# Strassen's seven products for an encoder layer's gate and up projections, in two passes of 1024 tokens

## The chip, the cores and the metric

The kernel runs on one core of one Trainium2 chip. The metric is the device time of one execution in microseconds (us), the median of several runs. A core has five engines that run side by side, each with its own instruction stream, and wait for each other by semaphores: TensorE (PE), VectorE (DVE), ScalarE (ACT), GpSimd (POOL) and SyncE (SP, which only issues transfers here). SBUF is the on-chip memory of 128 partitions, PSUM holds TensorE's results in 8 banks of 128 x 512 fp32.

## The reference

The layer has 2048 tokens of width 1024. After the mixers (windowed attention and a state-space branch) it ends like this:

```python
x = x + rmsnorm(merged @ w_out, norm_mix_post)
h2 = rmsnorm(x, norm_ffn_pre)
gate = h2 @ w_ffn_gate                      # 1024 -> 2816
up = h2 @ w_ffn_up                          # 1024 -> 2816
gp = jnp.pad(gate, ((0, 0), (1, 1), (0, 0)))
gate = gp[:, :-2] * conv_w[0] + gp[:, 1:-1] * conv_w[1] + gp[:, 2:] * conv_w[2] + conv_b
f = jax.nn.gelu(gate) * up
return x + rmsnorm(f @ w_ffn_down, norm_ffn_post)
```

Everything is fp32 in and out.

## The kernel before, in words

The kernel is a row of stages, each in its own block, with a barrier of all engines between them; what passes from one to the next goes through DRAM. In order: projection in, mixers, branches, output projection (`stage_out`, tiles named `ou_`), gate and up (`stage_gate_up`, `gu_`), down projection (`stage_down`, `dn_`).

Every large product is made of three fp32r matmuls (`split_products`, lines 324 to 326): both operands are split into a high part, rounded to fp32r, and a low part, the rest; high x high, low x high and high x low are added up in one PSUM bank. A split is one copy (the high part) and one subtraction (the low part), whose two inputs both lie in SBUF.

`stage_out` works through 16 tiles of 128 tokens. For each, SP loads 128 tokens of `merged`, ACT makes the high part and DVE the low part, PE does 48 matmuls (8 k, 2 halves of the width, 3 products). ACT then squares the result, POOL computes the inverse root in four small operations, DVE scales the rows and adds the residual, and POOL stores them to `x_mid`.

`stage_gate_up` starts with `NormTranspose`: SP loads 16 tiles of rows of `x_mid`, ACT squares, POOL makes the inverse root, DVE scales, PE transposes each tile in 8 pieces (line 253), and ACT (line 213) and DVE (line 234) keep the high and low parts of all 2048 tokens in SBUF. From the second group of four tiles on, the first block's product runs between the transposes. Then follows a loop over 22 row blocks of 128 of the 2816, each once for gate and once for up. `WeightStream` loads 128 columns of weights (512 KB), and DVE splits them (lines 314 and 316). PE computes four chunks of 512 tokens, each in its own bank, 24 matmuls to a bank. ACT copies gate's banks out (line 518), DVE runs the three taps of the convolution over 2048 tokens (lines 539, 542, 545), ACT applies gelu (line 522), DVE multiplies with up's banks (line 553), and POOL issues the store of the row block to `f` (line 571). ACT loads a function table each time it changes between copy and gelu. The four loads of the taps and the bias (lines 507 and 508) are the first things in ACT's stream. POOL has nothing in the loop but the 22 stores.

The order of work on each engine is the order of its code; nothing is planned at run time. PE's wait before a block is for the weights' low part, and before a bank for the one who reads it.

Of the kernel before, what the change touches and what calls it, by code (L numbers as in the profile page):

```python
# [28 lines left out]
P = 128  # L29
# [414 lines left out]
def stage_gate_up(nc, x_mid, gain, w_gate, w_up, conv_w, conv_b, f_scratch):  # L444


    with ExitStack() as ctx:
        m = Pool(nc, ctx, "gu")
        nt = NormTranspose(m, x_mid, gain)
        m.sb("shift", [P, 96])  # L450
        ws = WeightStream(m, KD)

        gate = m.sb("gate", [P, TOK + 2])
        conv = m.sb("conv", [P, TOK])
        taps = m.sb("taps", [P, 4, KF])
        banks = m.psum("banks", [P, 8, BANK])
        turn_psum = banks[:, 4:8, :].rearrange("p (s b) (k t) -> p s (b k) t", s=2, t=P)
        taps_in = m.sem("taps_in")
        edges_zero = m.sem("edges_zero")
        gate_read = m.sem("gate_read")  # L460
        up_read = m.sem("up_read")
        gate_free = m.sem("gate_free")
        tap = m.sem("tap")
        gelu_done = m.sem("gelu_done")
        stored = m.pool_dma_sem("stored")
        conv_free = m.sem("conv_free")
        f_rows = f_scratch.rearrange("(b p) t -> b p t", p=P)
        block = ctx.enter_context(nc.Block())

        @block.gpsimd  # L470
        def _(pool):
            pool.memset(gate[:, 0:1], 0.0).then_inc(edges_zero, 1)
            pool.memset(gate[:, TOK + 1:TOK + 2], 0.0).then_inc(edges_zero, 1)
            nt.gpsimd(pool)

        @block.sync
        def _(sync):
            nt.load(sync, ws, [(s, weights, slice(0, P)) for s, weights in enumerate((w_gate, w_up))])
            with sync.Fori(1, KF) as i:
                ws.load(sync, w_gate, 0, i * 2, bass.ds(i * P, P))  # L480
                ws.load(sync, w_up, 1, i * 2 + 1, bass.ds(i * P, P))

        @block.tensor
        def _(pe):
            def product(i, s):
                pe.wait_ge(ws.lo_ready, i * 2 + s + 1)
                for c in range(CHUNKS):

                    pe.wait_ge(up_read if s else gate_read, i * CHUNKS + c + 1)
                    for k in range(KD):  # L490
                        cols = slice(c * BANK, (c + 1) * BANK)
                        last = split_products(pe, banks[:, s * CHUNKS + c, :], ws.hi[:, s, k], ws.lo[:, s, k],
                                              nt.feat_hi[:, k, cols], nt.feat_lo[:, k, cols],
                                              k == 0, k == KD - 1)
                    last.then_inc(ws.chunk_done, 1)

            nt.tensor(pe, turn_psum, banks, ws)
            product(0, 1)
            with pe.Fori(1, KF) as i:
                for s in range(2):  # L500
                    product(i, s)

        @block.scalar
        def _(act):
            with nc.allow_non_contiguous_dma(reason="small"):
# [3 lines left out]
            nt.scalar(act, turn_psum)  # L509
            act.sem_inc(gate_read, CHUNKS)  # L510
            act.sem_inc(gelu_done, 1)
            act.wait_ge(taps_in, 64)
            with act.Fori(0, KF) as i:

                act.wait_ge(gate_free, i + 1)
                for c in range(CHUNKS):
                    ws.wait_chunk(act, i * 2, c)
                    act.activation(gate[:, 1 + c * BANK:1 + (c + 1) * BANK], banks[:, c, :], ACT.Copy)\  # L518
                        .then_inc(gate_read, 1)

                act.wait_ge(tap, i * 3 + 3)
                act.activation(conv[:], conv[:], ACT.Gelu_apprx_tanh, bias=taps[:, 3, bass.ds(i, 1)])\
                    .then_inc(gelu_done, 1)

        @block.vector
        def _(dve):
            nt.vector(dve, turn_psum, ws)
            dve.sem_inc(gate_free, 1)
            dve.sem_inc(up_read, CHUNKS)
            dve.wait_ge(taps_in, 64)  # L530
            dve.wait_ge(edges_zero, 2)
            dve.sem_inc(conv_free, 1)

            def finish(i):


                dve.wait_ge(gate_read, i * CHUNKS + 2 * CHUNKS)
                dve.wait_ge(conv_free, i + 1)
                dve.tensor_scalar(conv[:], gate[:, 0:TOK], taps[:, 0, bass.ds(i, 1)], None,
                                  ALU.mult).then_inc(tap, 1)  # L540
                dve.wait_ge(tap, i * 3 + 1)
                dve.scalar_tensor_tensor(out=conv[:], in0=gate[:, 1:TOK + 1], scalar=taps[:, 1, bass.ds(i, 1)],
                                         in1=conv[:], op0=ALU.mult, op1=ALU.add).then_inc(tap, 1)
                dve.wait_ge(tap, i * 3 + 2)
                dve.scalar_tensor_tensor(out=conv[:], in0=gate[:, 2:TOK + 2], scalar=taps[:, 2, bass.ds(i, 1)],
# [1896 lines left out]
```

## Time and profile before

| | us |
|---|---|
| median of the runs | 3066.26 (3 runs, 3066.14 to 3066.8) |
| span of the profiled execution | 3065.0 (no other time is given for that execution) |
| PE busy | 2799.5 (91%) |
| DVE busy | 1266.1 (41%) |
| ACT busy | 760.4 (25%) |
| POOL busy | 530.8 (17%) |
| output projection, from block start to the next | 1326.7 to 1526.7 |
| gate and up: start to last matmul | 1526.7 to 2545.1 |
| down projection | 2553.6 to the end |

The span goes from the first to the last instruction of one execution. Busy time of PE is drawn with each matmul's drain, so neighbouring matmuls overlap in the rows: what one costs is the distance between two starts. Stage borders are read from the first instruction of the next block.

### The profile page before, as it was taken

The numbers are of one execution on the slowest core, as the hardware profiler recorded it, in microseconds if no ns is written. First come the engines' busy times: TensorE is split into PE (matmuls) and PEld (weight loads), VectorE is DVE, ScalarE is ACT, GpSimd is POOL, SyncE is SP. The second block draws the span as 40 slices with busy tenths as digits, with TensorE's granted clock in tenths as the row PEclk, the third lists the DMA queues.
The fourth block names the chain that finished last, engine by engine and source line by source line (L and its number), as shares of the span: only waits on it lengthen the run. The fifth ranks groups of instructions, "written<-read, shape, count | busy, mean of one in ns | idle before, by whom it ended". The sixth has DMA issues, their size and how long they took to land. (4 is left out here: it accounts for less than half of the span.)

```text
span 3065.0 us, 35647 instructions
## 1 busy us (share of the span) xinstructions
PE 2799.5 (91%) x12942; PEld 2293.0 (75%) x12942; DVE 1266.1 (41%) x1448; ACT 760.4 (25%) x1200; POOL 530.8 (17%) x840
## 2 busy tenths in 40 slices
PE   6996999778988879979759999999999997999998
PEld 5885788666877667868648888888888885888886
DVE  5013664598696065433253232322223223224432
ACT  4111665522222150022141111111111113113221
POOL 2363220188880000001120000000000001000111
PEclk9997999899999989989979999999999998999999
DMA  5551324645555653355341111111111106334553
GB/s 158 161 203 57 75 66 101 176 150 157 186 175 191 119 195 139 149 172 144 118 129 55 34 55 48 55 34 55 48 54 38 51 34 199 94 98 146 170 169 118
DMA packets 375392, 350.66 MB, mean 114 GB/s; under 512 B 49552, under 2 KB 322960, under 8 KB 366480
## 3 DMA queue, kind: packets, MB, share of 16 engines
q1 hardware_dynamic: 326560, 227.93, 26.1%
q0 software_dynamic: 14352, 76.03, 6.9%
q10 hardware_dynamic: 34400, 45.67, 4.5%
q8 instruction: 47, 0.77, 0.1%
q14 instruction: 33, 0.27, 0.0%
HBM read 242.09 MB, written 107.48 MB: 114 GB/s over the span
## 5 line engine op out<-in xcount | busy, mean ns | idle before, releaser
L324 PE MATMUL gu_banks<-gu_feat_hi,gu_w_hi 128*128 128x512 f32 (+1 forms) x1408 | 549.8, 390 | 1.0 <-DVE gu_feat_lo L234 1.0
L326 PE MATMUL gu_banks<-gu_feat_lo,gu_w_hi 128*128 128x512 f32 (+1 forms) x1408 | 548.8, 390 | 0.0
L325 PE MATMUL gu_banks<-gu_feat_hi,gu_w_lo 128*128 128x512 f32 (+1 forms) x1408 | 548.5, 390 | 0.0
L324 PEld LDWEIGHTS gu_banks<-gu_feat_hi,gu_w_hi 128*128 128x128 f32 x1408 | 264.9, 188 | 55.7 <-DVE gu_feat_lo L234 1.4
L326 PEld LDWEIGHTS gu_banks<-gu_feat_lo,gu_w_hi 128*128 128x128 f32 x1408 | 264.8, 188 | 55.1
L325 PEld LDWEIGHTS gu_banks<-gu_feat_hi,gu_w_lo 128*128 128x128 f32 x1408 | 264.9, 188 | 54.6
L324 PE MATMUL dn_y<-dn_w_hi,dn_f_hi 128*128 128x512 f32 x704 | 276.1, 392 | 22.7 <-DVE dn_w_lo L815 22.6
L314 DVE CAST gu_w_hi<-gu_w_raw 128x1024 fp32r<-128x1024 f32 x44 | 30.5, 694 | 619.2 <-PE gu_banks L326 619.2
L325 PE MATMUL dn_y<-dn_w_hi,dn_f_lo 128*128 128x512 f32 x704 | 275.4, 391 | 0.0
L326 PE MATMUL dn_y<-dn_w_lo,dn_f_hi 128*128 128x512 f32 x704 | 275.2, 391 | 0.0
L518 ACT ACTIVATE gu_gate<-gu_banks 128x512 f32<-128x512 f32 x88 | 52.7, 601 | 596.3 <-PE gu_banks L326 596.2
L571 POOL DMA_DIRECT2D f<-gu_conv x22 | 11.8, 536 | 936.5 <-DVE gu_conv L553 936.5
L324 PEld LDWEIGHTS dn_y<-dn_w_hi,dn_f_hi 128*128 128x128 f32 x704 | 132.9, 189 | 52.5 <-issue 19.4
L326 PEld LDWEIGHTS dn_y<-dn_w_lo,dn_f_hi 128*128 128x128 f32 x704 | 133.1, 189 | 27.9
L325 PEld LDWEIGHTS dn_y<-dn_w_hi,dn_f_lo 128*128 128x128 f32 x704 | 133.1, 189 | 27.6
L2352 POOL TENSOR_TENSOR bases<-gs_states,bases 128x512 f32<-128x512 f32 (+2 forms) x90 | 109.6, 1218 | 202.9 <-POOLq L2373 179.6
L2238 ACT ACTIVATE gs_w_hi<-gs_w_raw 128x1024 fp32r<-128x1024 f32 x64 | 67.9, 1060 | 302.6 <-PE gs_banks L326 284.3
L763 ACT ACTIVATE dn_f_hi<-dn_f_raw 128x1408 fp32r<-128x1408 f32 x64 | 85.2, 1372 | 204.0 <-PE dn_y L326 163.0
L2272 DVE TENSOR_TENSOR gs_w_lo<-gs_w_raw,gs_w_hi 128x1024 fp32r<-128x1024 f32 x64 | 104.3, 1629 | 74.1 <-ACT gs_w_hi L2238 74.0
L324 PE MATMUL gs_banks<-gs_feat,gs_w_hi 128*128 128x512 f32 x256 | 104.8, 410 | 26.0 <-DVE gs_w_lo L2272 26.0
L324 PE MATMUL pi_banks<-pi_feat_hi,pi_w_hi 128*128 128x512 f32 (+1 forms) x320 | 126.2, 394 | 1.0 <-DVE pi_feat_lo L234 1.0
L326 PE MATMUL pi_banks<-pi_feat_lo,pi_w_hi 128*128 128x512 f32 (+1 forms) x320 | 125.1, 391 | 0.0
(259 smaller groups left out, 5066.7 us busy)
## 6 DMA issues: line engine op xcount, KB each, us to landing
dn_f_raw<-f SPq DMA_DIRECT2D x64, 704.0 KB, 5.7
gs_w_raw<-in_w_in SPq DMA_DIRECT2D x64, 512.0 KB, 4.5
f<-gu_conv POOLq DMA_DIRECT2D x22, 1024.0 KB, 4.2
gates<-gs_gate_out ACTq DMA_DIRECT2D x64, 256.0 KB, 3.0
br_rows<-gates POOLq DMA_DIRECT2D x16, 1024.0 KB, 6.9
gu_w_raw<-in_w_ffn_gate SPq DMA_DIRECT2D x22, 512.0 KB, 3.8
gu_w_raw<-in_w_ffn_up SPq DMA_DIRECT2D x22, 512.0 KB, 3.9
dn_w_raw<-in_w_ffn_down POOLq DMA_DIRECT2D x22, 512.0 KB, 6.0
```

The source lines that it names most:

```text
L314: dve.tensor_copy(self.hi[:, s], self.raw[:, s]).then_inc(self.hi_ready, 1)
L324: pe.matmul(out, w_hi, x_hi, start=first, stop=False)
L325: pe.matmul(out, w_lo, x_hi, start=False, stop=False)
L326: return pe.matmul(out, w_hi, x_lo, start=False, stop=last)
L518: act.activation(gate[:, 1 + c * BANK:1 + (c + 1) * BANK], banks[:, c, :], ACT.Copy)\
L571: pool.dma_start(f_rows[i], conv[:]).then_inc(stored, 16)
L763: act.activation(f_hi[:, s, h * KH:(h + 1) * KH], f_raw[:, h], ACT.Copy)\
L2238: act.activation(w_hi[:, n % 2], w_raw[:, n % 2], ACT.Copy).then_inc(w_hi_ready, 1)
L2272: dve.tensor_tensor(w_lo[:, n % 2], w_raw[:, n % 2], w_hi[:, n % 2].bitcast(F32), ALU.subtract)\
L2352: engine.tensor_tensor((by_re, by_im)[n], source, factor, ALU.mult).then_inc(done, 1)
```

## The change

The gate and up products are made by one level of Strassen's scheme, in Winograd's form. The weights of a pair of row blocks (256 columns) are cut into four quarters, A11 to A22, of 512 rows of k by 128 columns; the features of 1024 tokens into four, of 512 of k by 512 tokens. Seven products of 4 k x 3 matmuls give the four 128 x 512 results, where eight would be needed. For the weights POOL makes four sums and differences, two in place; for the features it makes 16 differences of 128x512, in place. SBUF has no room for the seven split right operands of all tokens, so the stage runs in two passes of 1024 tokens, each over 11 pairs and over gate and up: 44 units. The weights are loaded once in each pass.

The seven results share four banks of each kind: product 0 and 4 bank A, 1 and 5 bank C, 2 and 6 bank DD, 3 bank B; the later product of a bank is added to the earlier, after ACT has copied the earlier one out (products 0 and 1), or DVE has read it (product 2).

```diff
+HALF = TOK // 2
+KHALF = KD // 2
+PAIRS = KF // 2
+PER_PASS = 2 * PAIRS
+UNITS = 2 * PER_PASS
+OPS = 7
...
+            def product(u, j):
+                bank = banks[:, kind, (A, C, DD, B, A, C, DD)[j]]
+                pe.wait_ge(a_lo_ready, u * OPS + j + 1)
...
+                if j == 4:
+                    pe.wait_ge(p_one_kept, u + 1)
+                if j == 5:
+                    pe.wait_ge(p_five_kept, u + 1)
+                if j == 6:
+                    pe.wait_ge(u_three_ready, u + 1)
+                for k in range(KHALF):
+                    if u % PER_PASS == 0:
+                        pe.wait_ge(b_lo_ready, (p * OPS + j) * KHALF + k + 1)
+                    last = added_products(pe, bank, a_hi[:, j, k], a_lo[:, j, k], b_hi[:, j, k], b_lo[:, j, k],
+                                          j < 4 and k == 0, k == KHALF - 1, j >= 4)
```

POOL's stream (each difference of features waits for the split of what it overwrites, and the split of its result waits for it):

```diff
+            sum_one(0)
+            sum_three(0)
+            for k in range(KHALF):
+                difference_one(0, k)
+            sum_two(0)
+            for k in range(KHALF):
+                difference_three(0, k)
+            sum_four(0)
+            for k in range(KHALF):
+                difference_two(0, k)
+            for k in range(KHALF):
+                difference_four(0, k)
+            for u in range(UNITS):
+                turning = u == PER_PASS - 1
+                if u + 1 < UNITS:
+                    sum_one(u + 1)
+                    sum_three(u + 1)
...
+                if u % 2:
+                    times_up(u, 1, 1)
+                    times_up(u, 0, 1)
+                    up_edge(u)
+                    times_up(u, 1, 0)
+                if turning:
+                    for k in range(KHALF):
+                        difference_four(1, k)
```

ACT's stream (copies of products 0 and 1, gelu of one row block at a time, high parts):

```diff
+            for j in range(OPS):
+                split_a(0, j)
+                split_b(0, j)
             act.wait_ge(taps_in, 64)
+            for u in range(UNITS):
+                for j in range(OPS):
+                    if j == 0:
+                        keep_one(u)
+                    if j == 1:
+                        keep_five(u)
+                    if u % 2 and j in (3, 4):
+                        gelu(u, j - 3)
+                    if u % 2 == 0 and j == 4:
+                        keep_c11(u)
+                    if u + 1 < UNITS:
+                        split_a(u + 1, j)
+                    if u == PER_PASS - 1:
+                        split_b(1, j)
```

DVE's stream (low parts, the sums of the results, convolution of 1023 or 1025 columns for each of two row blocks):

```diff
+            for u in range(UNITS):
+                up, turning = u % 2 == 1, u == PER_PASS - 1
+                if up:
+                    convolve(u, 0)
+                split_a(u + 1, 0)
+                if turning:
+                    split_b(1, 0)
+                if up:
+                    convolve(u, 1)
+                split_a(u + 1, 1)
+                if turning:
+                    split_b(1, 1)
+                split_a(u + 1, 2)
+                u_two_three(u)
...
+                c22(u)
+                if up:
+                    up_c11(u)
+                split_a(u + 1, 4)
...
+                c12(u)
+                split_a(u + 1, 5)
...
+                c21(u)
+                if not up:
+                    edges(u)
+                split_a(u + 1, 6)
```

`split_a` is one operation of 128x512, `split_b` four of them. SP loads the weights by halves of k (512 KB each, a ring of three) and also issues the stores to `f` (1 MB, two row blocks of 1024 tokens). All of the stage's code is written out, without loops.

`stage_out` takes over the FFN's norm and transposes. For each tile, after the residual sum, ACT squares the rows, POOL makes three small operations, DVE scales (`norm_mid`), and PE transposes the tile two tiles later; ACT keeps the first 1024 tokens in SBUF (`feat_raw`), which stays for the next stage, and copies the others out and stores them to DRAM (`feat_late`), from where they are loaded in the first pass:

```diff
+            sync.dma_start(mid_gain[:], row_broadcast(ffn_gain)).then_inc(mid_gain_in, 16)
...
+            for t in range(TILES):
+                tile(t)
+                if t >= 2:
+                    turn_tile(t - 2)
+            turn_tile(TILES - 2)
+            turn_tile(TILES - 1)
...
+            for t in range(TILES):
+                act.wait_ge(y_done, t + 1)
+                pn.scalar(act, t, t % 2, [y[:, t % 2, 0], y[:, t % 2, 1]])
+                if t + 2 < TILES:
+                    split_hi(t + 2)
+                square_mid(t)
+                if t >= 2:
+                    keep_features(t - 2)
```

## Rows read from the trace of the kernel before

**Rows 1.** The page, part 1: busy us (share of the span) and instructions.
```profile
PE 2799.5 (91%) x12942; PEld 2293.0 (75%) x12942; DVE 1266.1 (41%) x1448; ACT 760.4 (25%) x1200; POOL 530.8 (17%) x840
```

**Rows 2.** Windows of gate/up: length, busy PE, PEld, DVE, ACT, POOL; PEclk, DMA, GB/s.
```profile
1526.70:1564.80 38.10, 8.82 (x40) 7.34 (x41) 14.16 (x12) 10.54 (x16) 7.63 (x25) 0.54 0.69 167
1564.80:1607.00 42.20, 34.15 (x177) 27.24 (x176) 28.73 (x24) 23.94 (x33) 9.36 (x30) 0.92 0.31 100
1607.00:2545.10 938.10, 938.08 (x4139) 776.70 (x4137) 266.58 (x237) 152.05 (x154) 11.26 (x21) 1.00 0.14 46
```

**Rows 3.** Timeline of PE (start, length): gate/up, 48 matmuls apart; mixers, 111 apart.
```profile
1730.28 0.39 PE L324 MATMUL gu_banks<-gu_feat_hi,gu_w_hi 128*128 128x512 f32 x1
1741.16 0.39 PE L324 MATMUL gu_banks<-gu_feat_hi,gu_w_hi 128*128 128x512 f32 x1
...
799.45 0.39 PE L324 MATMUL gs_banks<-sm_u_region,gs_w_hi 128*128 128x512 f32 x1
824.61 0.39 PE L324 MATMUL gs_banks<-gs_feat,gs_w_hi 128*128 128x512 f32 x1
```

**Rows 4.** Groups of instructions: count, busy us, mean ns, idle before and its releaser.
```profile
L316 DVE TENSOR_TENSOR br_w_lo<-br_w_raw,br_w_hi 128x512 fp32r<-128x512 f32 x20 | 13.8, 692 | 0.7
L1119 ACT ACTIVATE ou_g_hi<-ou_g_raw 128x1024 fp32r<-128x1024 f32 x16 | 16.9, 1056 | 185.8 <-DMA ou_g_raw<-merged 185.8
L522 ACT ACT_TABLE_LOAD x22 | 28.2, 1283 | 177.5 <-DVE gu_conv L545 177.5
L539 DVE TENSOR_SCALAR gu_conv<-gu_gate,gu_taps 128x2048 f32<-128x2048 f32 x22 | 28.3, 1286 | 26.1 <-ACT gu_gate L518 17.6 <-DVE gu_w_lo L316 8.4
L542 DVE SCALAR_TENSOR_TENSOR gu_conv<-gu_gate,gu_taps,gu_conv 128x2048 f32<-128x2048 f32 x22 | 51.7, 2352 | 3.2 <-DVE gu_conv L539 3.2
```

**Rows 5.** Timeline of POOL and DVE in the mixers; last, one group by form.
```profile
281.96 2.02 POOL L1434 TENSOR_TENSOR at_table_temp<-bases 128x1024 f32<-128x1024 f32 x1
639.99 4.30 DVE L2352 TENSOR_TENSOR bases<-gs_states,bases 128x512 f32<-128x512 f32 x2
645.73 1.82 DVE L2272 TENSOR_TENSOR gs_w_lo<-gs_w_raw,gs_w_hi 128x1024 fp32r<-128x1024 f32 x1
648.92 1.36 POOL L2352 TENSOR_TENSOR bases<-gs_states,bases 128x512 f32<-128x512 f32 x1 [0.18 <-POOL bases L2352]
654.38 1.83 DVE L2272 TENSOR_TENSOR gs_w_lo<-gs_w_raw,gs_w_hi 128x1024 fp32r<-128x1024 f32 x1
...
L2352 DVE TENSOR_TENSOR bases<-gs_states,bases 128x512 f32<-128x512 f32 x30 | 52.3, 1745 | 0.7
```

**Rows 6.** Timeline of ACT's queue: the last of its four loads of taps.
```profile
1541.02 2.06 ACTq L508 DMA_DIRECT2D gu_taps<-in_conv_b  x1
```

**Rows 7.** The page, part 6: transfers, KB each, median us from issue to landing.
```profile
dn_f_raw<-f SPq DMA_DIRECT2D x64, 704.0 KB, 5.7
f<-gu_conv POOLq DMA_DIRECT2D x22, 1024.0 KB, 4.2
gates<-gs_gate_out ACTq DMA_DIRECT2D x64, 256.0 KB, 3.0
gu_w_raw<-in_w_ffn_gate SPq DMA_DIRECT2D x22, 512.0 KB, 3.8
```

**Rows 8.** Timeline of PE: one of the first matmuls of gate/up.
```profile
1565.38 0.63 PE L325 MATMUL gu_banks<-gu_feat_hi,gu_w_lo 128*128 x1
```

**Rows 9.** Timeline of PE's weight loads: one tile's eight transposes.
```profile
1600.17 0.85 PEld L253 LDWEIGHTS gu_banks<-gu_ident,gu_normed 128*128 128x128 f32 x8 [1.49 <-issue]
```

**Rows 10.** Timeline at the ends of the output projection and of gate/up.
```profile
1519.49 1.23 DVE L644 TENSOR_TENSOR ou_rows<-ou_rows,ou_scaled 128x1024 f32<-128x1024 f32 x1
1526.79 0.33 SPq L163 DMA_DIRECT2D gu_rows<-x_mid  x1
...
2544.69 0.39 PE L326 MATMUL gu_banks<-gu_feat_lo,gu_w_hi 128*128 128x512 f32 x1
2553.59 1.13 SPq L698 DMA_DIRECT2D dn_f_raw<-f  x2
```

More of the change, by code:

```diff
@@ L441, in _, with added_products @@
                 act.wait_ge(stored[s], (n_blocks // 2) * 16 + 16)
-def stage_gate_up(nc, x_mid, gain, w_gate, w_up, conv_w, conv_b, f_scratch):
+HALF = TOK // 2
[4 more added lines that the diff above has]
+OPS = 7
+def added_products(pe, out, w_hi, w_lo, x_hi, x_lo, first, last, again):
+    pe.matmul(out, w_hi, x_hi, start=first, stop=False, skip_group_check=again)
+    pe.matmul(out, w_lo, x_hi, start=False, stop=False, skip_group_check=again)
+    return pe.matmul(out, w_hi, x_lo, start=False, stop=last, skip_group_check=again)
@@ L470, in _, with wait_raw @@
         @block.gpsimd
         def _(pool):
[L472 to L481, printed above, removed]
+            def wait_raw(u, h):
+                n = 2 * u + h
+                pool.wait_ge(raw_in[n % 3], n // 3 * 16 + 16)
@@ new lines, in keep_five, with keep_c11 @@
+            def keep_five(u):
+                act.wait_ge(product_done, u * OPS + 2)
+                if u:
+                    act.wait_ge(c22_done, u)
+                act.activation(p_five[:], banks[:, u % 2, C], ACT.Copy).then_inc(p_five_kept, 1)
+            def keep_c11(u):
+                _, _, g = place(u)
+                act.wait_ge(product_done, u * OPS + 5)
+                if g:
+                    act.wait_ge(tap, g * 6)
+                act.activation(out_of(u, 0, 0), banks[:, 0, A], ACT.Copy).then_inc(gate_c11_done, 1)
@@ L505, in _, with gelu @@
+            def gelu(u, e):
+                p, pair, g = place(u)
+                act.wait_ge(tap, g * 6 + 3 * e + 3)
+                size = HALF - 1 + 2 * p
+                act.activation(conv[:, e, 0:size], conv[:, e, 0:size], ACT.Gelu_apprx_tanh,
+                               bias=taps[:, 3, 2 * pair + e:2 * pair + e + 1]).then_inc(gelu_done, 1)
             with nc.allow_non_contiguous_dma(reason="small"):
@@ new lines, in convolve @@
+            def convolve(u, e):
+                p, pair, g = place(u)
+                if e == 0:
+                    dve.wait_ge(gate_c11_done, g + 1)
+                    dve.wait_ge(edge_kept, g + 1)
+                    if g:
+                        dve.wait_ge(stored, g * 16)
+                size = HALF - 1 + 2 * p
+                out = conv[:, e, 0:size]
+                weight = [taps[:, j, 2 * pair + e:2 * pair + e + 1] for j in range(3)]
+                first = g * 6 + 3 * e
+                dve.tensor_scalar(out, gate[:, e, 0:size], weight[0], None, ALU.mult).then_inc(tap, 1)
+                for j in range(1, 3):
+                    dve.wait_ge(tap, first + j)
+                    dve.scalar_tensor_tensor(out=out, in0=gate[:, e, j:j + size], scalar=weight[j], in1=out,
+                                             op0=ALU.mult, op1=ALU.add).then_inc(tap, 1)
@@ L530, in _ @@
+            for j in range(OPS):
+                split_a(0, j)
+                split_b(0, j)
             dve.wait_ge(taps_in, 64)
             dve.wait_ge(edges_zero, 2)
[L532 to L545, printed above, removed]
-                                         in1=conv[:], op0=ALU.mult, op1=ALU.add).then_inc(tap, 1)
@@ L1103, in tile, with turn_tile @@
                 done.then_inc(y_done, 1)
-            pe.sem_inc(y_done, 2)
-            tile(0, 0, first=True)
-            tile(0, 1)
-            with pe.Fori(1, TILES // 2) as i:
-                for s in range(2):
-                    tile(i, s)
+            def turn_tile(t):
+                s = t % 2
+                pe.wait_ge(mid_ready, t + 1)
+                if t >= 2:
+                    pe.wait_ge(feat_copied, t - 1)
+                for k in range(KD):
+                    turn = pe.transpose(turn_psum[:, s, k, :], mid_normed[:, s, k * P:(k + 1) * P], ident[:])
+                turn.then_inc(turned, 1)
```

481 lines of the change are left out of this document (363 added, 118 removed).

## The prediction, made before the changed kernel was run

> **What bounds the kernel now.** I read the page's engine totals first: PE multiplies 2799.5 us of 3065.0 (91%); DVE, next after PE's own weight loads, has 41% on the page [rows 1]. The reader is to see there that only fewer matmuls, or fewer holes between them, can move the time. Next the windows by stage: from 1607 to 2545 us, the gate/up loop, PE has 938.08 busy us in 938.10 at granted clock 1.00 with DVE at 28%, ACT at 16% and POOL at 1%; before it stand 38.1 us in which PE does 8.8 and 42.2 in which it does 34 [rows 2]. Then the timeline of PE inside the loop: two matmuls 48 places apart start 10.88 us apart, so one costs 0.2267 us whatever its own row says (0.39, drawn with its drain) [rows 3]. The chain that ended last shows only the down projection, so it decides nothing here. In this loop time is the count of matmuls times 0.2267, as long as the others keep up; that is what the rest asks.
>
> **The products.** Before: 44 blocks x 4 banks x 8 k x 3 = 4224 matmuls. After: 44 units (22 pair-halves of gate and up, two passes) x 7 products x 4 k x 3 = 3696. One unit is 84 x 0.2267 = 19.04 us, a product 2.72 us. The code of PE is now straight-line; in the gate products of the mixers, whose code is too, 111 matmuls take 25.16 us, 0.2267 each [rows 3]: I take 0 for it.
>
> **Does an ordinary unit keep PE fed?** Prices [rows 4]: the low part of a 128x512 split on DVE 0.69, and I take the same for an add or a product of 512 columns; the high part on ACT 0.57 (1.056 for 1024 columns, and half the columns leave a little over half), a PSUM copy 0.6 and a gelu of 1024 columns 1.1 at the same rate, a table load 1.28, taps of 1025 columns 0.7 and twice 1.28 (from 1.286 and 2.352 for 2048), semaphore gaps 0.15. A gate unit costs DVE 7 splits and 5 adds, 8.3 us; an up unit adds the two convolutions (7.1) and one product: 16 us. ACT has 5.9 and, with two gelus and four table loads, 13.2. All below 19.04. The splits of unit u+1 follow unit u's product of the same number, 16 us ahead of their use. The tight wait is the seventh product, which takes the bank of product 3 only when U3 has been added. In an up unit DVE does, from its start: C21 and the edge of the unit before (1.1), a split (1.8), convolution (5.3), split, convolution (9.6), two splits (11.0), U2 and U3: 12.6 us; the product wants it at 6 x 2.72 = 16.3. Waiting behind that pair on DVE are four splits and C22, and POOL's products behind C22; none is wanted for 10 us. ACT's keep copies run at 2.7 and 5.4 us, wanted at 10.9 and 13.6.
>
> What can eat the 3.7 us is POOL. It gets 8 sums and 3 products of 128x512 in two units, which nobody did there before. The trace has such a neighbourhood: while the scan runs on POOL, two 128x512 adds on DVE take 4.30 us instead of 1.38 (1.745 is their mean over the stage); POOL's 1024 columns alone take 2.02, so 512 about 1.05. From one gs_w_lo to the next (645.73 to 654.38) the two engines' work without company, about 3.3 and 4.6 us, fills 8.65 [rows 5]. They take turns. In the up unit two of POOL's sums fall ahead of U3: 2 x 1.3 puts it at 15.2. Margin 1.1 us; the unit holds. The Trainium skill, "SBUF — State Buffer", section "Who interferes with whom", has the rule: a VectorE instruction with two SBUF inputs and a GpSimd instruction that reads SBUF exclude each other for the whole instruction. The trace agrees (0.69 becomes about 2.0, the price of both in turn); by the rule alone a contested pair would cost 0.69 + 1.05 = 1.74, and the prologue below would be 5 us shorter.
>
> **The start of the stage.** Before: stage start 1526.72, last matmul done at 2545.1: 1018.4 us. ACT issues the four tap loads first, to 1543.1 [rows 6]; they stay first, so its first split comes 16.4 us in, with the weights (3.8 us landing [rows 7]) long there. Then all seven right operands are made: 28 + 7 splits on ACT (20 us) and DVE, and 16 + 2 in-place differences on POOL that each wait for a split and are waited for by one. Contested: 18 x 2.0 = 36, and 17 splits more at 0.69 = 11.7; from 17.2 to about 65 us. The fifth product waits for ACT's keep copy, which is queued behind the last of ACT's 35 splits, and the seventh for U3, behind the last of DVE's and three more: 65 + 2.1 + 1.4 = 68.5, and 2.7 for the product. Unit 0 ends 72 us in. Ends: 50 if the two engines don't exclude each other (POOL's chain alone, 18 x 1.2 from 18.6 on, then two splits, the keep copy and three products, with 2 us for gaps), 82 if each of its handovers costs twice the 0.15 us.
>
> **The turn of the passes.** In unit 21 the 28 splits and 16 differences come again, among the unit's own. DVE reaches U3 of unit 21 after 11 splits and both convolutions, with ten of POOL's operations between: about 31 us in, wanted at 16.3: 15 us. Then the order of POOL: its last four differences stand behind unit 21's last product with up, which waits for C21 on DVE, behind 15 more splits: they end near 55 us, the last split of ACT behind them, and behind that the keep copy of unit 22, which its fifth product wanted at 45.6: 11 to 12 us. I take 27 in all; 12 without exclusion, 40 at the other end. Reloading the late features (4 MB on SP's queue, issued at half-tile 10 of 88) has hundreds of us. After the idle start of the old stage the granted clock is 0.54 in the mean [rows 2], near 1.2 of 2.4 GHz, and the first matmuls are drawn with 0.63 instead of 0.39 [rows 8]; for such restarts I take 2 us together.
>
> New stage, start to last matmul: 72 + 43 x 19.04 (818.7) + 27 + 2 = 919.7 against 1018.4: **98.7 less**.
>
> **The output projection.** PE is paced there as well: tiles of 48 matmuls, 10.88 us. Eight transposes take 0.86 us until the next matmul [rows 9]; 13 tiles' worth fall before the last tile ends: 11.2 us more. DVE's added norm (1.28) and ACT's square and copy (2.3) leave both under 6 us of 11.8 a tile. The gain row is 512 KB more on SP's queue while the weights still arrive and ACT waits for them: 1.5 (0 to 3). At the end, before: sum done 1520.7, store issued, next stage 1526.7 [rows 10]. After: square 1.25, POOL's three steps 1.2, norm 1.28, transposes 2 (at the lower clock), copy 1.03, then 512 KB to DRAM with 512-byte runs, 4.5 (3.0 for 256 KB, 5.7 for 704 KB [rows 7]), and the barrier as before, 1.3: 1533.5, so 7 more (5 to 9). The input DMAs, waiting in SP's queue for the rows of two tiles earlier, have 15 us to spare. **19.7 more.**
>
> **The end of gate/up.** After the last matmul now: product 0.69, store on POOL, landing 4.2, next stage at 2553.6 [rows 7, 10]. After: C21 0.69, POOL's product 1.1, SP's issue of the same 1 MB: **1.2 more**.
>
> **Sum.** -98.7 + 19.7 + 1.2 = -77.8 us. The span is 3065.0; the profile has no other time for its execution, and the median of the runs shown is 3066.26, 1.3 above the span. 3066.3 - 77.8 = 2988.5: **2988.5 us**, 2.5% faster.
>
> **Rivals.** (a) *Engines don't exclude each other here*: most of POOL's operands are contiguous and each short, and one of its scan operations of 512 columns took 1.36 [rows 5]. Start at 50, turn at 12: 37 us less, 2951. Against it: the 4.30 for two. 0.15. (b) *U3 late in up units*: if tensor_scalar of an odd length runs at one element a cycle (0.4 more each, twice) and a third contested pair falls in, U3 stands at 17.3 to 18.3: 1 to 2 us in each of 22 up units, 22 to 44 us: 3010 to 3033. For it: a margin of 1.1. Against: POOL's next sum waits for that very split. 0.17. (c) *DVE and POOL together become the bound, and it is slower than before*: two units give DVE 24 us of work, of which 16 instructions contend. At the scan's mean of 1.745 for each and the convolutions blocked as often, 45 us against 38.1: 7 us a pair, 22 pairs, +154: 3142. It decides against the change from 3.5 us a pair. Against it: POOL is busy 13 us in 38, not always as in the scan, so it can't block DVE for 21. 0.10. (d) *Start and turn far longer*, above 80 and 45, from a chain of waits I have not seen: 3020 to 3066. 0.05.
>
> **Chances.** Forecast 0.53, with a range of its own of 2968 to 3012 (the start's and turn's ends, in part cancelling); (a) 0.15, (b) 0.17, (c) 0.10, (d) 0.05. The range takes (a), the forecast and most of (b): 2948 to 3045. A change of 0.2%, 6 us, is what a measurement can tell from none. Slower is (c), 0.10; within 0.2% is the last part of (d), 0.02; faster is the rest, 0.88.
>
> **What would show it.** In the changed profile: matmuls of gate/up 0.2267 apart and 19.0 us from one unit's first to the next's; the first matmul 18 us after the stage's start and the eighth product 72 after it; POOL's 128x512 rows near 1.2 alone and 1.9 in the start; a hole of 15 us before unit 21's seventh product, waiting for DVE, and one of 11 before unit 22's fifth, waiting for ACT; the output projection 11 longer between first and last matmul. The forecast is wrong if PE has a hole in every up unit (then (b) or (c)), or if the start takes under 60 or over 85 us.

## The result, and the profile after

The changed kernel takes 2973.88 us (median of 4 runs, 2973.55 to 2974.55) against 3066.53 beside it: ratio 0.9698, interval 0.9684 to 0.9712, so 3.0% faster. Forecast were 2988.5, and 2948 to 3045 as the range. A hole, below, is idle time of PE just before a matmul.

The page, part 1, of the changed kernel (answers to [rows 1]): PE has 105 us less to do, DVE 371 and POOL 383 more.

```profile
PE 2694.6 (91%) x12414; PEld 2199.8 (74%) x12414; DVE 1636.8 (55%) x1950; ACT 933.3 (31%) x1565; POOL 913.8 (31%) x1111
```

Windows of the changed kernel: output projection (its first 5 us still belong to the stage before), unit 0, units 1 to 20, the turn, the second pass, the down projection (columns as in [rows 2]):

```profile
1326.70:1545.97 219.27, 191.80 (x896) 159.35 (x896) 90.70 (x89) 77.12 (x136) 43.02 (x133) 0.94 0.51 163
1545.97:1607.60 61.63, 35.09 (x84) 22.50 (x85) 49.47 (x45) 24.55 (x44) 39.58 (x26) 0.64 0.29 50
1607.60:2000.00 392.40, 392.40 (x1733) 324.92 (x1732) 279.52 (x332) 141.09 (x222) 163.52 (x125) 1.00 0.29 93
2000.00:2062.00 62.00, 39.20 (x156) 31.51 (x155) 56.55 (x58) 25.76 (x44) 40.77 (x27) 0.83 0.16 51
2062.00:2453.40 391.40, 391.40 (x1728) 323.79 (x1726) 271.93 (x326) 134.70 (x210) 154.54 (x121) 1.00 0.24 77
2453.40:2972.10 518.70, 483.07 (x2113) 398.08 (x2112) 180.33 (x151) 127.26 (x150) 44.76 (x106) 0.97 0.50 147
```

There are two kinds of stretch. In the third and the fifth PE is never idle at clock 1.00: 41 of the 44 units cost their matmuls and nothing else. In the second and the fourth DVE is busy 80% and 91% of the time and PE waits. All that PE waits for there (line, releaser: us in total, times, longest; 7.4 more stand in the output projection's tail):

```profile
PE gu_banks L454 <- DVE gu_b_lo L812: 24.6, 5, 18.0
PE gu_banks L454 <- issue: 14.5, 2, 10.8
PE gu_banks L454 <- DVE gu_gate L831: 12.0, 1, 12.0
PE ou_turn L1496 <- DVE ou_mid_normed L1570: 7.4, 1, 7.4
PE gu_banks L454 <- ACT gu_u_two L754: 3.5, 1, 3.5
```

The account, by starts. The output projection's first load is issued at

```profile
1327.84 1.00 SPq L1068 DMA_DIRECT2D ou_g_raw<-merged  x2
```

in the kernel before and at

```profile
1331.83 1.01 SPq L1436 DMA_DIRECT2D ou_g_raw<-merged  x2
```

in the changed one: +4.0 us from the stages ahead of it, whose code is the same in both. In the profiled executions of all the kernels of this document that issue lies between 1326.3 and 1332.9, so such a difference says nothing of the change. (The block begins at 1327.8, and not at 1326.7 as the table of the time before has it.) The output projection then takes 214.1 us against 199.0 (+15.2), and gate/up begins at 1545.97 against 1526.72 (+19.3 in all); from there to the last matmul 907.1 against 1018.0 (-110.9); from there to the down projection 7.8 against 8.9 (-1.1). Sum -92.7; the down projection takes 0.2 less, and the spans differ by 92.9 (3065.0 to 2972.1). Below, "stage" is the length from the stage's start to its last matmul in the profiled execution; times are compared by ratio to the kernel before on the same chip (3067 to 3068 there, so 0.001 is 3 us).

### The profile page after: what moved, and what is told of

The parts are those of the page before. It is cut to its first block and busy times, and to the rows that moved or that the text cites. A ratio compares the mean times of both kernels' runs of the same rounds, so it can differ in the third digit from the quotient of the medians.

```text
span 2972.1 us, 35255 instructions
## 1 busy us (share of the span) xinstructions
PE 2694.6 (91%) x12414; PEld 2199.8 (74%) x12414; DVE 1636.8 (55%) x1950; ACT 933.3 (31%) x1565; POOL 913.8 (31%) x1111
## 5 line engine op out<-in xcount | busy, mean ns | idle before, releaser
L454 PE MATMUL gu_banks<-gu_b_hi,gu_a_hi 128*128 128x512 f32 x1232 | 488.0, 396 | 54.7 <-DVE gu_b_lo L812 24.6
L456 PE MATMUL gu_banks<-gu_b_lo,gu_a_hi 128*128 128x512 f32 x1232 | 485.3, 394 | 0.0
L455 PE MATMUL gu_banks<-gu_b_hi,gu_a_lo 128*128 128x512 f32 x1232 | 485.1, 394 | 0.0
L454 PEld LDWEIGHTS gu_banks<-gu_b_hi,gu_a_hi 128*128 128x128 f32 x1232 | 234.6, 190 | 112.0 <-issue 39.4
L456 PEld LDWEIGHTS gu_banks<-gu_b_lo,gu_a_hi 128*128 128x128 f32 x1232 | 234.7, 191 | 50.0
L455 PEld LDWEIGHTS gu_banks<-gu_b_hi,gu_a_lo 128*128 128x128 f32 x1232 | 235.2, 191 | 48.1
L806 DVE TENSOR_TENSOR gu_a_lo<-gu_raw,gu_a_hi 128x512 fp32r<-128x512 f32 x220 | 199.8, 908 | 116.3 <-ACT gu_a_hi L738 116.3
L738 ACT ACTIVATE gu_a_hi<-gu_raw 128x512 fp32r<-128x512 f32 x220 | 138.6, 630 | 259.2 <-PE gu_banks L456 234.5
L880 DVE SCALAR_TENSOR_TENSOR gu_conv<-gu_gate,gu_taps,gu_conv 128x1023 f32<-128x1023 f32 (+1 forms) x88 | 134.1, 1524 | 3.1
L642 POOL TENSOR_TENSOR gu_conv<-gu_conv,gu_gate 128x512 f32<-128x512 f32 (+1 forms) x66 | 96.6, 1463 | 124.3 <-DVE gu_gate L837 58.9
```

The lines of the kernel that those rows point to most:

```text
L454: pe.matmul(out, w_hi, x_hi, start=first, stop=False, skip_group_check=again)
L455: pe.matmul(out, w_lo, x_hi, start=False, stop=False, skip_group_check=again)
L456: return pe.matmul(out, w_hi, x_lo, start=False, stop=last, skip_group_check=again)
L642: pool.tensor_tensor(mine, mine, factor, ALU.mult).then_inc(up_done, 1)
L738: act.activation(a_hi[:, j], a_source(u, j), ACT.Copy).then_inc(a_hi_ready, 1)
L806: dve.tensor_tensor(a_lo[:, j], a_source(u, j), a_hi[:, j].bitcast(F32), ALU.subtract)\
```

## The experiments

U2 and U3 are two sums that DVE makes one after the other: U2 from ACT's copy of product 0 and the bank of product 3, U3 from U2 and the bank of product 2. A unit's seventh product goes into that last bank, so it waits for U3.

The theory: an ordinary unit costs 84 x 0.2267; the whole gain is 528 matmuls less; the price stands in unit 0 and at the turn, where DVE and POOL take turns. The rivals were (a) no exclusion, (b) U3 late, (c) DVE and POOL as the bound, and that the gain comes from something else, the norm's move above all.

### Is it the matmuls? (e1_eighth_product)

```diff
-                for k in range(KHALF):
+                for k in [*range(KHALF)] * (2 if j == 3 else 1):
```

> Product 3 of every unit is computed twice (its bank starts anew), so a unit has 96 matmuls as four plain banks would; all else is the changed kernel's. Theory (an ordinary unit lasts as long as its matmuls): 44 x 12 x 0.2267 = 119.7 us more than the changed kernel's 2973.9, less up to 5 us that fall into the holes of the first unit: 3089 to 3094, slower than the kernel before. Rival (other engines set the pace of a unit, and the gain came from the shorter start): less than 60 us more, under 3034.

Measured 3086.68, ratio 1.0062 (1.0045 to 1.0079), stage 1020.1: 112.8 more than the changed kernel, which is 113.0 by the stage alone, and 2.3 below the range expected. With an eighth product the new scheme is slower than the kernel before. The 119.7 of the added matmuls are not all seen because some of them fill holes: those of the turn, of which the expectation had taken no account, shrink from 12.0 and 10.8 to 9.3 and 7.9, by a product's 2.72 each or a little more.

### What does the norm's move give alone? (e7_norm_alone, e7b_norm_alone)

Both have the eight products and loops of before; the features come ready from the output projection. They differ in one place of ACT's stream:

```diff
+            act.sem_inc(gate_read, CHUNKS)
+            act.sem_inc(gelu_done, 1)
             for c in range(CHUNKS):
...
-            act.sem_inc(gate_read, CHUNKS)
-            act.sem_inc(gelu_done, 1)
             act.wait_ge(taps_in, 64)
```

> One part alone: the output projection with the FFN's norm and transposes as in the changed kernel, and gate/up with four plain banks as before, fed from the kept and the stored features. Theory (the gain is the matmuls saved; moving the norm gives back most of what it takes): output projection 19 us longer, gate/up's start 60 us of lost time down to about 15 (taps 10.4, first splits 1.2, lower clock 2): 25 to 30 us less than before, 3036 to 3042. Rival (the norm's move carries the larger share of the 93 us): under 3020. Rival (it only costs): over 3066.

> Eight products as before the change, with the norm of the features made inside the output projection, as in e7_norm_alone; only the release of the PSUM banks of the gate (gate_read) now stands ahead of ScalarE's feature splits instead of behind them. Theory: in e7_norm_alone the first matmul waited 37.0 us in one hole for ScalarE's queue although its operands stood ready about 21 us earlier, so this order takes about 21 us off: 3034 to 3040 us, the first matmul of gate and up near 1553 and not at 1574, the stage from there as long as before. Against the kernel before that is 26 to 32 us faster by the move of the norm alone. Rival: the features' splits on VectorE, not the release, set the first matmuls, and the hole is broken into waits for feature splits of the same sum: 3050 to 3060 us.

The first missed: 3057.86, ratio 0.9972 (0.9962 to 0.9981). ACT released the PSUM banks only behind all its splits, and PE stood:

```profile
1574.28 0.77 PE L324 MATMUL gu_banks<-gu_feat_hi,gu_w_hi 128*128 128x512 f32 x1 [37.03 <-ACTq L525]
```

With the release ahead of the splits the same row is

```profile
1553.73 0.76 PE L324 MATMUL gu_banks<-gu_feat_hi,gu_w_hi 128*128 128x512 f32 x1 [16.24 <-DVE gu_feat_lo L552]
```

and the time 3038.82, ratio 0.9909 (0.9892 to 0.9925), as expected: the norm's move alone is worth 28 us, and Strassen's scheme the other 65 (each ratio is good to some 5 us). Its stage is 975.5; 957.5 of it are matmuls (4224 x 0.2267), 18 overhead. The changed kernel has 837.9 of matmuls and 69.2 of overhead. So the scheme takes off 119.7 and gives back 51 at the start and the turn.

### What do the differences cost? (e2_no_differences, e3_write_only)

e2 puts a semaphore increment in the place of each of POOL's 32 feature differences; e3 has in the first pass a `memset` of 1400 columns in the place of each (`pool.memset(conv...[:, 0:1400], 0.0)`), about as long (1.36 us from start to start), but reading nothing.

> POOL's 32 differences of features are left out (a semaphore increment stands in their place, so all waits and their order stay); the products are then of wrong operands. Theory (in the start and at the turn POOL's differences and DVE's splits exclude each other and add up): the start falls from 62 us to about 41 (35 splits on DVE 0.61 apart from 11 us on, then U2, U3 and a product), the turn's two holes of 12.0 and 10.8 us nearly vanish: 40 to 45 us less than 2973.9, 2929 to 2934. Rival (the start is set by ACT's and DVE's own splits, the differences lie beside them): 0 to 10 us less, 2964 to 2974.

> In the first pass each of the 16 differences of features is replaced by a memset of 1400 columns of a tile that is not in use yet: about as long on POOL (1.25 us) but reading nothing; the products of that pass are of wrong operands. Theory (exclusion by POOL's reading): DVE's splits in the start come down from 1.68 us apart to 0.61 where they have their inputs, POOL's rows from 1.7 to about 1.3 each, and the start is then POOL's chain: 62 us falls to 47 to 50, the whole to 2959 to 2962. Rival (POOL's chain of waits and its own speed set the start, DVE is only late behind it): POOL's rows stay near 1.7, time within 3 us of 2973.9.

e2: 2940.08, ratio 0.9589 (0.9573 to 0.9605), stage 874.6: 32.5 less, and short of the 40 to 45 expected. Unit 0 ends 46.2 us in and not 61.6, where 41 was meant; the two units of the turn last 47.9 us for 65.0, and 38.1 would be without any loss. e3: 2959.57, ratio 0.9650 (0.9634 to 0.9666), stage 896.5: 10.6 less, and the time as expected; all of it is at the start (unit 0 ends 51.2 us in, a little above the 47 to 50 expected; U3 of unit 0 at 47.5 us into the stage instead of 56.4), with the turn's holes unchanged at 12.0 and 10.9. POOL has about the same time to spend in e3; only its reads are gone. DVE's and POOL's rows of the changed kernel in unit 0, and DVE's for the same line in an unhindered stretch, show the price:

```profile
1564.04 6.79 DVE L812 TENSOR_TENSOR gu_b_lo<-feat_raw,gu_b_hi 128x512 fp32r<-128x512 f32 x4
1566.88 6.76 POOL L624 TENSOR_TENSOR feat_raw<-feat_raw 128x512 f32<-128x512 f32 x4
...
1597.48 2.48 DVE L812 TENSOR_TENSOR gu_b_lo<-feat_raw,gu_b_hi 128x512 fp32r<-128x512 f32 x4
```

From the start of such a row to the start of the next one on DVE (1570.76 and 1599.89, not shown) four pairs take 6.72 us, 1.68 a pair; alone four DVE operations take 2.40, 0.60 each. Rival (a) falls.

### Do the taps hold the start? (e4_taps_on_sync)

The four small loads leave the head of ACT's queue for SP's, behind the third load of weights:

```diff
                 load_half(n)
+                if n == 2:
+                    for j in range(3):
+                        sync.dma_start(taps[:, j, :], conv_w[j].rearrange("(b p) -> p b", p=P)).then_inc(taps_in, 16)
+                    sync.dma_start(taps[:, 3, :], conv_b.rearrange("(b p) -> p b", p=P)).then_inc(taps_in, 16)
```

> The changed kernel with the four small loads of the convolution's taps issued from SyncE's queue behind the third load of weights instead of from the head of ScalarE's queue. Theory: ScalarE spent its first 10.5 us of the stage on issuing them (8.4 and 2.0 us) and its first split began only then; now it begins at +6.5 or so (behind its wait for the operand), and since the operands of unit 0 set the end of unit 0, the stage is 3 to 6 us shorter: 2968 to 2971 us. Rival: VectorE's and GpSimd's pace (1.68 us for a pair that meets on their operands) sets the start, not ScalarE's first split: within 1.5 us of the changed kernel, 2972.5 to 2975 us. Third: SyncE's queue is held by the issue and loads of weights come late, slower by 2 us or more.

2968.5, ratio 0.9678 (0.9662 to 0.9694), against 0.9698: the intervals overlap, but the stage says it: 902.9, 4.2 less, as expected. ACT's first split starts 3.9 us in and not 10.5, the first matmul 6.0 and not 12.6 in; 4.7 of that is left at the end of unit 0; the rest goes into waits for DVE's splits.

### Is the turn a matter of order? (e5a_difference_four, e5b_both_holes)

```diff
                     for k in range(KHALF):
                         difference_two(1, k)
+                    for k in range(KHALF):
+                        difference_four(1, k)
                 if u % 2:
...
-                if turning:
-                    for k in range(KHALF):
-                        difference_four(1, k)
```

and in e5b, on DVE's stream:

```diff
                 split_a(u + 1, 0)
-                if turning:
-                    split_b(1, 0)
                 if up:
                     convolve(u, 1)
+                if turning:
+                    split_b(1, 0)
+                    u_two_three(u)
```

> The changed kernel with one move at the turn between the passes: GpSimd's difference for the fifth operand (the four rows of difference_four) stands ahead of its products with up instead of behind them. Theory: the second hole of the turn (10.8 us, ScalarE's keep copy behind its split of operand 6, which waits for that difference) goes, and part of the lower clock after it; the first hole (12.0 us, which waits for VectorE's gate of 2x2 sums, U3) stays: 11 to 13 us less than the changed kernel, 2961 to 2963 us. Rival: the hole only moves, since the products with up that are now later hold VectorE's convolution or the end of the unit: no less than 3 us gained, and a hole of 8 us or more on another releaser.

> The move of e5a_difference_four, and besides: at the turn VectorE makes the second convolution before its first split of the new pass, and the sum U3 right after that split; at the start of the stage ScalarE's two keep copies of unit 0 stand after its fourth split, and VectorE's sum U2/U3 of unit 0 after its fifth split, not behind all seven. Theory: both holes of the turn (12.0 and 10.8 us) and the clock lost behind them go, and 3 to 6 us of the start: 24 to 28 us less than the changed kernel, 2946 to 2950 us. Rival: the splits that are moved back become the late ones (a hole on a split of the new pass of 6 us or more at the turn): 2955 to 2963 us.

Both missed. e5a: 2970.05, ratio 0.9681 (0.9665 to 0.9697), stage 906.5. e5b: 2973.39, ratio 0.9692 (0.9676 to 0.9708), stage 908.6. The stage gains 0.6 us in e5a and loses 1.5 in e5b. What PE waits for after 2010 us, first in e5a, then in e5b:

```profile
2015.01 0.77 PE L454 MATMUL gu_banks<-gu_b_hi,gu_a_hi 128*128 128x512 f32 x1 [11.96 <-DVE gu_gate L830]
2037.37 0.76 PE L454 MATMUL gu_banks<-gu_b_hi,gu_a_hi 128*128 128x512 f32 x1 [5.72 <-DVE gu_a_lo L805]
2047.17 0.47 PE L454 MATMUL gu_banks<-gu_b_hi,gu_a_hi 128*128 128x512 f32 x1 [2.19 <-issue]
```

```profile
2013.94 0.76 PE L454 MATMUL gu_banks<-gu_b_hi,gu_a_hi 128*128 128x512 f32 x1 [2.50 <-DVE gu_b_lo L814]
...
2037.91 0.77 PE L454 MATMUL gu_banks<-gu_b_hi,gu_a_hi 128*128 128x512 f32 x1 [11.73 <-ACT gu_u_two L753]
2047.69 0.54 PE L454 MATMUL gu_banks<-gu_b_hi,gu_a_hi 128*128 128x512 f32 x1 [2.55 <-issue]
```

The holes are broken up and get new names, but their sum is still 20 us (19.9 in e5a; 20.3 in e5b with four short ones that are not shown; 22.8 in the changed kernel), and what is gained there is lost in matmuls at the lower clock: the two units of the turn, 38.1 us without loss, last 65.0 us in the changed kernel and in e5a, 65.6 in e5b. At the start, e5b's unit 0 ends 56.2 us in for 61.6, but a hole of 3.7 on U3 comes up in unit 1, and unit 2 begins 0.9 later than in the changed kernel. DVE is full meanwhile. e5a's window of the turn:

```profile
2000.00:2062.00 62.00, 42.12 (x156) 33.36 (x155) 59.98 (x58) 26.40 (x44) 40.84 (x26) 0.81 0.16 51
```

59.98 us of 62.00 (e5b has the same): here the turn lasts as long as DVE's work does, what POOL holds it up among it. In e2, where POOL has no differences, the holes there were 2.5 and 4.5. The releasers of the two holes were real, and moving what they waited for was worth nothing.

### Take work off that pair (e9a_differences_dve, e9b_all, e10_sum_first)

e9a moves the four `difference_*` functions from POOL's stream to DVE's, word for word, behind the split that each waits for (`differences(p, j)` is one and three behind split 0, two behind 1, four behind 3):

```diff
                 split_b(0, j)
+                differences(0, j)
...
                     split_b(1, 0)
+                    differences(1, 0)
```

e9b adds e4's taps and this order of DVE's turn, behind its first split and difference; besides, ACT's keep copies of unit 22 stand ahead of the split of operand 6, those of unit 0 behind the fifth split, U2/U3 of unit 0 behind the sixth:

```diff
+                    convolve(u, 1)
+                    split_a(u + 1, 1)
+                    u_two_three(u)
+                    for k in range(KHALF):
+                        difference_three(1, k)
+                    split_b(1, 1)
+                    differences(1, 1)
+                    split_a(u + 1, 2)
+                    split_b(1, 2)
+                    c22(u)
+                    up_c11(u)
+                    c12(u)
+                    c21(u)
+                    for j in range(3, OPS):
+                        split_a(u + 1, j)
+                        split_b(1, j)
+                        differences(1, j)
```

and e10 moves `u_two_three(22)` ahead of `split_a(23, 1)`.

> The changed kernel with the 32 differences of features (16 at the start, 16 at the turn) made by VectorE in its own queue, right behind the split that each waits for, instead of by GpSimd. Nothing is left out and nothing else is moved. Theory after e5a and e5b, where a hole of the turn only changed its place: VectorE is full there (59.98 of 62.00 us busy), and what sets both the start and the turn is its own work plus 1.08 us for each GpSimd difference that it meets (1.68 for the pair against 0.60 alone). A difference on VectorE costs 0.60, so 16 of them are about 8 us less of VectorE's time in each place, and what waits for them gets them sooner: the gate of 2x2 sums U3 of unit 0 at about 1590 and not 1602.4, the start 9 to 12 us shorter; the holes of the turn (22.8 us together) 8 to 14: in all 18 to 28 us less than the changed kernel, 2946 to 2956 us. Rival: the two engines do not hinder each other and VectorE's added 16 x 0.60 = 9.6 us per place come on top, 10 to 19 us slower: 2984 to 2993 us. Second rival: order and not VectorE's load sets the turn, then the start alone gives 9 to 12: 2962 to 2965 us.

> e9a_differences_dve and e4_taps_on_sync together, and an order of the turn made for VectorE's load: U2/U3 of unit 21 ahead of the second operand's split, its four outputs ahead of the fourth operand's split, ScalarE's two keep copies of unit 22 ahead of the split of operand 6; at the start the keep copies of unit 0 behind ScalarE's fifth split and U2/U3 of unit 0 behind VectorE's sixth. Theory: the taps' 4 to 5 us and some 4 to 8 us of the turn and start come on top: 2935 to 2945 us. If order does not matter: e9a less 5.

> e9b_all with one more move: in unit 22, the first after the turn, VectorE makes U2/U3 ahead of the second and third splits of the next unit's weights, not behind them. In e9b_all the last hole of the turn (8.4 us, on the gate of 2x2 sums U3) came because VectorE waited there for ScalarE's split of a weight sum that GpSimd got done only after a row of back-to-back VectorE operations, and U3 stood behind it. Theory: GpSimd's late sum no longer holds U3, which comes some 5 us sooner: 4 to 7 us less than e9b_all with the lower clock behind the hole, 2945 to 2949 us. Rival: the weight splits themselves are then late for unit 23 and the hole comes back there: within 2 us of e9b_all.

e9a: 2959.44, ratio 0.9654 (0.9638 to 0.9670), stage 893.8, 13.3 less: 7.4 at the start and 5.9 at the turn. The direction is the theory's (the rival "10 to 19 slower" falls), the size is not, and the time is 3.4 above the range expected. At the turn the holes are 9.9, 2.1 and 2.5, 14.5 together for 22.8. At the start U3 of unit 0 comes 50.6 us in for 56.4, where 44 was meant. What ate the rest, POOL and ACT in unit 0 of e9a:

```profile
1561.32 17.23 POOL L615 TENSOR_TENSOR gu_s_one<-gu_raw 128x512 f32<-128x512 f32 x1 [7.32 <-DVE gu_a_lo L765]
...
1578.58 0.63 ACT L697 ACTIVATE gu_a_hi<-gu_s_one 128x512 fp32r<-128x512 f32 x1 [9.32 <-POOL gu_s_one L615]
```

One sum of 1.26 us lies 17.23 us on POOL while DVE's rows follow one another without a gap (from 1561.09 to 1577.4). ACT waits 9.3 for it, with two splits and the keep copy behind it, and PE 11.1 for that copy. e9b: 2952.3, ratio 0.9624 (0.9608 to 0.9640), stage 886.5; above the 2945 expected, for the same cause: its last hole, 8.4 on U3, goes back to ACT waiting 9.6 for such a sum. e10 takes U3 out from behind it: that hole is 3.7, the stage 882.3, 4.2 shorter, as expected; the time, 2950.22, ratio 0.9621 (0.9605 to 0.9637), is 1.2 above the range and does not tell it from e9b. So order is worth something again here: in e9b's turn DVE is busy 53.2 us of 57.8, since it waits there, and in e10's 52.1 of 53.6. e10 beats both kernels: 3.8% less than before, 0.8% less than the changed one.

### How near was the bound? (e6_more_pool_work)

Four additions ahead of `sum_two`, as here, and three behind it:

```diff
+                if u % 2 and not turning:
+                    for n in range(0, 4):
...
+                        pool.tensor_tensor(spare[:], b_hi[:, 0, 0].bitcast(F32), b_hi[:, 0, 1].bitcast(F32), ALU.add)
```

> The changed kernel with seven more additions of 128x512 on GpSimd in each up unit but that of the turn (four ahead of sum_two, three behind it; they read b_hi and write a tile that nobody reads): work added, nothing left out. It asks how near the ordinary units were to the bound by VectorE and GpSimd. Theory: an addition costs both engines 1.68 us where they meet, U3 of an up unit comes at about 21 us where it is wanted at 16.3, so each of 21 up units gets a hole of 3 to 6 us: 63 to 126 us more than the changed kernel, 3037 to 3100 us, about the time before the change. Rival: GpSimd takes the idle time of VectorE (280 of 392 us busy) and U3 does not move by more than its slack of 3.6 us: 2972 to 2978 us.

3090.74, ratio 1.0080 (1.0063 to 1.0097), stage 1027.2, 120.1 more: slower than the kernel before, though before the addition POOL was busy 42% and DVE 71% of the ordinary units (third window above). Twenty of the 21 up units with additions get a hole on U3 (the stage's last unit has none); the second of them, and the windows behind the first:

```profile
1669.00 0.77 PE L454 MATMUL gu_banks<-gu_b_hi,gu_a_hi 128*128 128x512 f32 x1 [3.64 <-DVE gu_gate L846]
```

```profile
1624.20:1630.30 6.10, 6.10 (x15) 4.81 (x16) 5.81 (x7) 1.23 (x2) 3.52 (x3) 0.51 0.30 89
1630.30:1662.00 31.70, 31.70 (x141) 26.25 (x140) 20.98 (x22) 10.47 (x18) 20.11 (x15) 1.00 0.51 183
```

The twenty holes are 74.4 us. The rest of the 120 is the clock: behind the first, which ended at 1624.20, PE runs 6.1 us at the granted 0.51 (1.2 of 2.4 GHz), 3.0 us lost, nearly the hole again. Not behind every one: two up units are 38.08 us apart without holes, and the first ten holes lie 44.80 to 41.98 apart, so that 0.3 to 3.1 us are lost behind each, 2.3 on the average, which makes 46 of the 120. Rival (c) is a real mechanism; it just had not been reached.

## Why the prediction was right

**Products and ordinary units: right.** 41 units of 19.04 us without a hole. The margin of U3 in an up unit was larger than said: the unit that begins at 1645.9 has U3 done at 1658.6, 12.7 us in, wanted at 16.3; 15.2 was allowed for POOL's turns. Two things were not foreseen: POOL's two sums hit DVE there for 0.9 us in all, not 2.6; and ACT loads its table once in the stage, where I had charged four loads of 1.28 in every up unit (two groups of 22 before, one of them in [rows 4]; e7b, with the loops of before, has both groups again).

**The start: right in kind, 10.4 us too long** (72 against 61.6, and only 1.6 above the 60 below which the forecast was to count as wrong; it is the largest part of the error). Three terms of the sum were mis-sized. ACT's issue of the taps ended 10.5 us in and not 16.4 [rows 6], 5.9 us; why it was quicker is open. A contested pair costs 1.68 and not 2.0; 18 of them are 5.8 us. And the last product of the unit, put at 2.7 us, took 4.4, for behind its hole of 3.7 us most of it ran at the lower clock: 1.7 the other way. The seventh product could start 57.2 us in and not 68.5. I had taken the pair's price from the mixers' two additions in 4.30 [rows 5]. The Trainium skill, "SBUF — State Buffer", section "Who interferes with whom", calls the port pair that the two engines share an exclusive lock, by which, as an estimate, a pair costs the sum of the two operations' own durations, 1.74 by my figures; the prediction set that aside, and the measured 1.68 is nearer to it than to 2.0. That it is so near is in part luck: by this trace's own 0.60 and 1.26 the sum is 1.86. The lower end of the start, 50, adds up to 52 by its own terms.

**The turn: right**, 26.8 against 27 + 2, but in part by errors that cancel. The holes were 12.0 for 15 (ten of POOL's operations, 0.3 too dear each, would be that difference) and 10.8 for 11 to 12 (by its own terms the fifth product of unit 22 was wanted at 44.6, not 45.6), 22.8 together for 27; the lower clock behind them took 4.0, and 1.7 more at the end of unit 0, where 2 was put for both. They came at the products forecast; the first names DVE as releaser, as forecast, the second names none ("issue"), and ahead of that product stands ACT's keep copy, as forecast:

```profile
2016.85 0.77 PE L454 MATMUL gu_banks<-gu_b_hi,gu_a_hi 128*128 128x512 f32 x1 [11.96 <-DVE gu_gate L831]
...
2042.45 0.58 ACT L754 ACTIVATE gu_u_two<-gu_banks 128x512 f32<-128x512 f32 x1
...
2043.13 0.76 PE L454 MATMUL gu_banks<-gu_b_hi,gu_a_hi 128*128 128x512 f32 x1 [10.84 <-issue]
```

What the prediction read from them was only half right: it told the turn as two waits in a queue's order. e5a and e5b show that another order gains nothing, with DVE full; e9a and e2, which take work from it, shorten the turn by 5.9 and 17.1.

**Output projection: 4.5 us too long**, +15.2 against +19.7. That the next stage begins 19.3 later is no confirmation: 4.0 of it stand ahead of the projection, in unchanged stages. Between its first and its last product matmul there are 12.6 more, for 11.2; the tail behind them is 5.0 longer, for 7; and the first matmul comes 2.4 sooner (9.0 us in for 11.5), where the gain row was to make it 1.5 later. Why it comes sooner is open. **The end** of the stage is 1.1 shorter and not 1.2 longer: 2.3.

**Sum.** Too long were the stage by 12.2 (10.4 start, 2.2 turn, less 0.4 for the last matmul's own length), the projection by 4.5, the end by 2.3: 19.0 us. The stages ahead, put at nothing, took 4.0 more in the profiled execution; that leaves 15.0, against 14.6 found (2988.5 less 2973.9). So 4 us of the small error are chance. One more thing stands in the forecast's sum without a name: the old stage's 60.8 us beside its matmuls (1018.4 less 957.6) fall away with the norm's move. The theory ahead of the experiments called the 528 matmuls the whole gain; e7b shows that the move alone gives 28 of the 93 us. The largest part is the start, and in it the price of the contested pair, whose cause e3 confirms, and the taps that e4 shows to lie on the path.

**The rivals.** (a) fell with e2 and e3, (b) with the third and fifth window, (d) with the second and the fourth. (c) is the one that e6 brings about, with seven more operations in an up unit. Open is why holes of nearly the same 3.7 us in e6 cost between 0.3 and 3.1 us of lower clock.

## What to carry to other kernels

A scheme that saves matmuls is worth its count times their pitch wherever the helpers keep up, and its price stands at the few places where all operands change at once; count those apart. Where the engine that feeds PE is busy 90% of such a stretch, the releaser of a hole names the last item of a queue and not the cause: in e5a and e5b reordering only renamed the holes, and in e2, e3 and e9a work or blocking taken away shortened the stretch. Order counts again where that engine has waits of its own, as e10 shows. The spare time of an engine says little when its neighbour excludes it; 1.7 us a pair and the slack of one wait decide.

## What the runs showed of the hardware

- A short POOL operation that reads SBUF can be kept waiting far beyond one DVE instruction: 17.23 us for 1.26 in e9a, 17.25 and 6.97 in e10, each time under gapless DVE operations with two SBUF inputs. When both streams are dense they alternate instead, one pair in 1.68.
- Four DVE operations of 128x512 in 2.48 us, 0.60 each, where the row of one is drawn with 0.69 [rows 4]: sums of drawn rows overstate DVE.
- A `tensor_scalar` of 1023 columns takes 0.74 us, a little over half of the 1.286 for 2048 [rows 4]; an odd length costs nothing that shows, though no row here has 1024 columns to compare.
- A hole of 3.7 us on PE costs between 0.3 and 3.1 us more at the lower clock behind it.
